# RWKV triangles beside the projections, 32x32 blocks inverted on GpSimd, decay in the transposes

## The reference

```python
def step(state, inp):
    r_t, w_t, k_t, v_t, av_t, bv_t = inp
    sa = jnp.einsum('bhvk,bhk->bhv', state, av_t)
    state = (state * w_t[:, :, None, :] + sa[..., None] * bv_t[:, :, None, :]
             + v_t[..., None] * k_t[:, :, None, :])
    return state, jnp.einsum('bhvk,bhk->bhv', state, r_t)
...
_, y = lax.scan(step, s0, xs)
```

## Time and profile before

| | us |
|---|---|
| median of 3 runs | 3227.96 (3223.63 to 3230.2) |
| the profiled execution | 3227.73 |
| its span, first to last instruction | 3226.4 |
| PE busy | 3011.9 (93%) |
| DVE busy | 1792.1 (56%) |
| ACT busy | 1269.2 (39%) |
| POOL busy | 69.0 (2%) |

### The profile page before, as it was taken

The page is one execution under the profiler, slowest core; times in us unless marked ns, Lnnn a source line. Parts: engine busy times, 40 slices in busy tenths (PEclk is TensorE's granted clock), DMA queues, the critical chain, the costliest instruction groups (busy, mean ns, idle before and its releaser), DMA issues. The chain is left out here.

```text
span 3226.4 us, 65777 instructions
## 1 busy us (share of the span) xinstructions
PE 3011.9 (93%) x27928; PEld 2412.8 (75%) x27928; DVE 1792.1 (56%) x3385; ACT 1269.2 (39%) x2310; POOL 69.0 (2%) x36
## 2 busy tenths in 40 slices
PE   8998999999988999999999999898989899999998
PEld 6666777766667777767777777788878887778876
DVE  3566566523475245565654565556666665453465
ACT  4354343321244455555544444322222225443233
POOL 0000000000000001111100000000000000000000
PEclk9998999999999999999999999999999999999999
DMA  3000111242145522223233423431212225431114
GB/s 116 20 20 27 40 46 53 66 147 80 61 124 157 159 57 78 74 74 80 72 80 111 137 85 132 160 128 36 80 32 90 75 75 202 137 116 52 33 59 150
DMA packets 143972, 284.23 MB, mean 88 GB/s; under 512 B 43312, under 2 KB 84288, under 8 KB 142144
## 3 DMA queue, kind: packets, MB, share of 16 engines
q1 hardware_dynamic: 143680, 280.04, 27.5%
HBM read 222.79 MB, written 57.21 MB: 87 GB/s over the span
## 5 line engine op out<-in xcount | busy, mean ns | idle before, releaser
L234 PE MATMUL ps<-xs,wparts 128*128 128x512 f32 x1664 | 694.3, 417 | 12.0 <-DVE xs L1494 9.5
L236 PE MATMUL ps<-xs,wparts 128*128 128x512 f32 x1664 | 654.0, 393 | 0.0
L235 PE MATMUL ps<-xs,wparts 128*128 128x512 f32 x1664 | 652.8, 392 | 0.0
L302 DVE TENSOR_TENSOR wparts<-wring,wparts 128x1024 fp32r<-128x1024 f32 x248 | 303.9, 1225 | 311.7 <-ACT wparts L294 286.8
L234 PEld LDWEIGHTS ps<-xs,wparts 128*128 128x128 f32 x1664 | 313.3, 188 | 126.1 <-issue 63.7
L294 ACT ACTIVATE wparts<-wring 128x1024 fp32r<-128x1024 f32 x248 | 263.1, 1061 | 276.9 <-PE ps L236 214.3
L236 PEld LDWEIGHTS ps<-xs,wparts 128*128 128x128 f32 x1664 | 312.6, 188 | 71.2
L235 PEld LDWEIGHTS ps<-xs,wparts 128*128 128x128 f32 x1664 | 313.8, 189 | 60.7 <-issue 4.5
L2271 ACT ACTIVATE Pm<-Pm,ml 128x128 f32<-128x128 f32 (+1 forms) x384 | 168.4, 441 | 147.9 <-DVE ml L2339 147.8
L2339 DVE CUSTOM_DVE_ANT_0 Pm<-ps,mask 128x128 f32<-128x128 f32 (+1 forms) x384 | 110.8, 347 | 186.7 <-PE ps L2174 186.7
L2647 ACT ACTIVATE M<-ps 128x256 f32<-128x256 f32 x160 | 61.5, 384 | 258.5 <-PE ps L2446 249.9
(11 more groups left out here) (400 smaller groups left out, 5407.8 us busy)
## 6 DMA issues: line engine op xcount, KB each, us to landing
wring<-in_wo SPq DMA_DIRECT2D x96, 512.0 KB, 3.6
ops<-rw SPq DMA_DIRECT2D x32, 640.0 KB, 6.1
wring<-in_w SPq DMA_DIRECT2D x39, 512.0 KB, 3.5
wring<-in_w2u SPq DMA_DIRECT2D x33, 512.0 KB, 4.2
wring<-in_wg SPq DMA_DIRECT2D x24, 512.0 KB, 3.6
wring<-in_w2v SPq DMA_DIRECT2D x24, 512.0 KB, 4.2
wring<-in_w2a SPq DMA_DIRECT2D x24, 512.0 KB, 6.4
MB<-wst SPq DMA_DIRECT2D x48, 256.0 KB, 5.1
```

The source lines that it names most:

```text
L234: nc.tensor.matmul(out, a, c, start=start, stop=False)
L235: nc.tensor.matmul(out, b, c, start=False, stop=False)
L236: return nc.tensor.matmul(out, a, d, start=False, stop=stop)
L302: K.nc.vector.tensor_tensor(W.part(i, 1), W.raw(i), W.part(i, 0).bitcast(F32), ALU.subtract).then_inc(*K.dve.done("w_lo", W.first + i))
```

## The change

1. **The triangle Bc x AR moves into the projections.** `triangles_pe` does it for pair p-1 beside the units of the next group, four quarters q of 16 products each, three rounds apart; `triangles_dve` masks each quarter into one buffer `mbs`, and `mb_store` on SP writes it to DRAM ("mx"). The DVE instruction of a quarter waits until the store of the quarter before has landed. The last pair's four quarters come behind the units.
2. **GpSimd inverts the 32x32 diagonal blocks.** `solve_move` on SP gathers the 64 blocks of a pair into 64 partitions by four DMAs (runs of 128 bytes). `solve_pool` does 30 steps, each a multiplication and an addition over s x (31-s) elements. `xt_store` writes the inverses back by four DMAs. `solve_move` of pair p first waits for POOL's pair p-1 and stores it. Pairs 0 to 5 have it behind the weight loads 13, 17, 21, 25, 29 and 32; pair 6 between the first loads of the recurrence and the last `prep_store`; pair 7 inside the recurrence. A load of a piece needs its pair's `xt_store`.
3. **PE keeps one corner.** Per piece and stream, instead of five levels there are eight 32x32 products (`m1_mm`), two short ACT copies, eight more (`xt_mm`), a DVE transpose (`x11`) and one masked DVE copy of 128x128.
4. **The decay goes into the turns.** Kc and Bc are turned with a diagonal dg that holds the decay (four ACT instructions of 128x64), so L2768 goes and the state takes one instruction.
5. **The rounds.** Each piece has twelve rounds for chain and stage, the second stream's stage a round later, and `finish` is spread over four pieces.

```diff
     for p in range(NP):
         for i in range(4 * p + 3 if p else 6, 4 * p + 7):
             if i < 33:
                 yield from w_load(K, B.W, i)
+            if i in MB_AT:
+                yield from mb_store(K, A, B, MB_AT.index(i))
+            if i in SOLVE_AT:
+                yield from solve_move(K, A, B, SOLVE_AT.index(i))
         if p:
             yield from prep_store(K, A, B, p - 1)
+    yield from mb_store(K, A, B, NP - 2)
     yield from rwkv_first_sp(K, A, B.rw)
+    yield from solve_move(K, A, B, NP - 2)
     yield from prep_store(K, A, B, NP - 1)
+    yield from mb_store(K, A, B, NP - 1)
+    sp.wait_ge(*(yield "mb_store", NP - 1, 3))
     for p in (NP - 2, NP - 1):
         sp.wait_ge(*(yield "rw_store", p, "b"))
     barrier(K, sp, 3)
...
+MB_AT, SOLVE_AT = [12, 16, 20, 24, 28, 31], [13, 17, 21, 25, 29, 32]
+def mb_store(K, A, B, p):
+    for q in range(4):
+        K.sp.wait_ge(*(yield "m_b", p, q))
+        if p == 0 and q == 0:
+            K.sp.wait_ge(*(yield "mb_zero"))
+        K.nc.sync.dma_start(A["mx"][p][:, 4 * q:4 * q + 4, :], B.mbs).then_inc(*K.sp.done("mb_store", p, q, by=16))
...
+def xt_store(K, A, B, p):
+    K.sp.wait_ge(*(yield "solved", p))
+    for i, here, there in corners(A, B, p, 128):
+        K.nc.sync.dma_start(there, here).then_inc(
+            *K.sp.done("xt_part", p, i, by=16, also=[("xt_store", p)] if i == 3 else []))
+def solve_move(K, A, B, p):
+    K.sp.wait_ge(*(yield "mb_store", p, 3))
+    if p:
+        yield from xt_store(K, A, B, p - 1)
+        K.sp.wait_ge(*(yield "xt_store", p - 1))
+    for i, here, there in corners(A, B, p, 0):
+        K.nc.sync.dma_start(here, there).then_inc(
+            *K.sp.done("g_part", p, i, by=16, also=[("g_load", p)] if i == 3 else []))
...
+    G = B.G[0:64, :].rearrange("p (i t) -> p i t", t=32)
+    pool.wait_ge(*(yield "g_load", p))
+    pool.in_order()
+    nc.gpsimd.memset(B.G[0:64, 0:1024:33], 1.0).then_inc(*pool.done("one_diag", p))
+    for s in range(1, 31):
+        n = 31 - s
+        d = B.tmp[0:64, 0:s * n].rearrange("p (i t) -> p i t", t=n)
+        pool.in_order()
+        nc.gpsimd.tensor_tensor(d, G[:, 0:s, s:s + 1].to_broadcast([64, s, n]),
+                                G[:, s:s + 1, s + 1:32].to_broadcast([64, s, n]), ALU.mult).then_inc(
+            *pool.done("step_mul", p, s))
+        pool.in_order()
+        nc.gpsimd.tensor_tensor(G[:, 0:s, s + 1:32], G[:, 0:s, s + 1:32], d, ALU.add).then_inc(
+            *pool.done("step_add", p, s, also=[("solved", p)] if s == 30 else []))
...
+    for q in range(4):
+        bank, old = B.RM.take(("mb_mm", p, q), ("m_b", p, q))
+        pe.wait_ge(*(yield "prep", p))
+        pe.wait_ge(*(yield old))
+        for c in range(4 * q, 4 * q + 4):
+            a = tiles(nc, bank[:, half(c % 4, 128)], Bc[:, c, :], AR[:, c, :])
+        a.then_inc(*pe.done("mb_mm", p, q))
+        for _ in range(3):
+            yield STEP
...
+def triangles_dve(K, B, p):
+    nc, dve = K.nc, K.dve
+    for q in range(4):
+        dve.wait_ge(*(yield "mb_mm", p, q))
+        if q:
+            dve.wait_ge(*(yield "mb_store", p, q - 1))
+        elif p:
+            dve.wait_ge(*(yield "mb_store", p - 1, 3))
+        else:
+            dve.wait_ge(*(yield "mar"))
+        dve.in_order()
+        nc.vector.tensor_tensor(B.mbs[:, :, 0:128], K.bank["mb_mm", p, q].rearrange("p (c t) -> p c t", c=4),
+                                B.mar[:, :].unsqueeze(1).to_broadcast([128, 4, 128]), ALU.mult).then_inc(
+            *dve.done("m_b", p, q))
+        for _ in range(3):
+            yield STEP
...
+    gens = [in_turn(*[exactly(ROUNDS, chain(K, B, s, n)) for n in range(4 * NJ)]) for s in range(2)]
+    gens += [in_turn(*[exactly(ROUNDS, later(s, stage(K, B, s, n))) for n in range(1, 4 * NJ)]) for s in range(2)]
+    gens += [later(4 * ROUNDS, in_turn(*[exactly(4 * ROUNDS, later(2 * s, finish(K, B, s, j, SPREAD)))
+                                         for j in range(NJ - 1)])) for s in range(2)]
+    if split:
+        gens.append(later(3 * ROUNDS + 1, in_turn(*[exactly(ROUNDS, split(K, B, k)) for k in range(8, 16)])))
+    yield from weave(*gens)
...
-            if j and n == 4 * j + ND:
-                for s in range(2):
-                    yield from fin_store(K, A, B, s, j - 1)
+            yield from ops_load(K, A, B, s, n)
+        if n == 4:
+            yield from solve_move(K, A, B.prep, NP - 1)
+        if n == 8:
+            yield from xt_store(K, A, B.prep, NP - 1)
+            K.sp.wait_ge(*(yield "xt_store", NP - 1))
+            yield from mix_load(K, A, B, 15)
+        if n in (10, 14):
+            yield from finished_sp(K, A, B, n // 4 - 2)
+    yield from finished_sp(K, A, B, NJ - 2)
...
+    LT, _, XT = triangles(B, s, n)
+    XM = B.XM[:, s]
+    bank, old = B.RG.take(("mk_mm", s, n), ("m_k", s, n))
+    if old:
+        pe.wait_ge(*(yield old))
+    for c in range(4):
+        a = tiles(nc, bank[:, half(c, 128)], K4[:, c, :], AR[:, c, :])
+    a.then_inc(*pe.done("mk_mm", s, n))
+    yield STEP
+    yield STEP
+    bank, old = B.RG.take(("side_t", s, n, 0), ("side", s, n, 0))
+    if old:
+        pe.wait_ge(*(yield old))
+    turned(K, B, bank, V4, lambda c: B.stack).then_inc(*pe.done("side_t", s, n, 0))
+    yield STEP
+    yield STEP
+    bank, old = B.RG.take(("m1_mm", s, n), ("m1", s, n))
+    pe.wait_ge(*(yield "x11", s, n))
+    if old:
+        pe.wait_ge(*(yield old))
+    for c in range(4):
+        a = corner(nc, bank[:, half(c, 32)], LT[:, c, 32:64], XM[:, c, :], 0)
+    a.then_inc(*pe.done("m1_mm", s, n))
+    yield STEP
+    yield STEP
+    for x, src in ((1, K4), (2, B4)):
+        bank, old = B.RG.take(("side_t", s, n, x), ("side", s, n, x))
+        pe.wait_ge(*(yield "dg", s, n))
+        turned(K, B, bank, src, lambda c: B.dg[:, s, c, :]).then_inc(*pe.done("side_t", s, n, x))
+        if x == 1:
+            yield STEP
+            yield STEP
+            bank, old = B.RG.take(("xt_mm", s, n), ("xt", s, n))
+            pe.wait_ge(*(yield "m1", s, n))
+            if old:
+                pe.wait_ge(*(yield old))
+            for c in range(4):
+                a = corner(nc, bank[:, half(c, 32)], XM[:, c, :], XT[:, c, 32:64], 1)
+            a.then_inc(*pe.done("xt_mm", s, n))
+            yield STEP
+            yield STEP
...
+    dve.wait_ge(*(yield "ops_load", s, n))
+    dve.in_order()
+    nc.vector.transpose(XM[:, :, :], XT[:, :, 0:32]).then_inc(*dve.done("x11", s, n))
...
-        dve.wait_ge(*(yield state_key(s, n, c)))
-        dve.in_order()
-        nc.vector.tensor_scalar(d, B.ST[:, s, i, :], pc, None, ALU.mult).then_inc(*dve.done("r_decay", s, n, c))
...
-        nc.vector.scalar_tensor_tensor(B.ST[:, s, 1 - i, :], K.bank["w_mm", s, n, c][:, 0:64], pc, d, ALU.mult,
-                                       ALU.add).then_inc(*dve.done("r_state", s, n, c))
-        yield STEP
```

More of the change, by code:

```diff
@@ L214, in drive, with exactly @@
         assert moved, [asked[e] for e in live]
+def exactly(n, gen):
+    done = 0
+    x = next(gen, None)
+    while x is not None:
+        if x is STEP:
+            done += 1
+            yield STEP
+            x = next(gen, None)
+        else:
+            v = yield x
+            try:
+                x = gen.send(v)
+            except StopIteration:
+                x = None
+    assert done <= n, (done, n)
+    for _ in range(n - done):
+        yield STEP
 def later(steps, gen):
@@ L2630, in rwkv_first_pe @@
     K.pe.wait_ge(*(yield "c2c"))
-    yield from weave(*[stage_pe(K, B, s, 0) for s in range(2)], steps=True)
+    yield from weave(*[later(s, stage_pe(K, B, s, 0)) for s in range(2)], steps=True)
 def rwkv_pe(K, A, B):
@@ L2667, in chain_act @@
     j, g = divmod(n, 4)
-    for _ in range(12):
+    for _ in range(ROUNDS):
         yield STEP
@@ L2688, in finish_act @@
         *act.done("y_sq", s, j))
-    for _ in range(3):
+    for _ in range(sum(at[2:4])):
         yield STEP
@@ L2789, in finish_dve, with rounds @@
     bc = lambda x: x.unsqueeze(2).to_broadcast([128, 16, 64])
-    for _ in range(s):
-        yield STEP
+    def rounds(*which):
+        for _ in range(sum(at[i] for i in which)):
+            yield STEP
+    yield from rounds(0)
     dve.wait_ge(*(yield "y_out", s, 4 * j + 3))
```

318 lines of the change are left out of this document (162 added, 156 removed).

## The result

The changed kernel takes 3073.1 us (median of 4 runs, 3068.8 to 3085.3) against 3227.8 for the kernel before. The ratio is 0.9528, with a 95% interval of 0.9499 to 0.9558, so it is 4.7% faster. The forecast was 3097, in a range of 3010 to 3200. The profiled execution, the shortest of the four, took 3068.8 us, and its span is 3067.4, 159.0 us shorter than before.

The account below looks back on a forecast made before the run. The recurrence was taken as bounded by PE's instruction count, DVE's big instructions second. 3226.4 + 56 (projections) + 31 (transition) - 217 (recurrence) = 3096, with 1.3 us around the span 3097; range 3010 to 3200.

Parts of the forecast that it names:

- its own case: Whole kernel: the predicted costs and gain hold as summed, 3097 us, within 3050 to 3150; chance 0.50.
- Projections: Seven projection groups: each pays 4.9 us of PE's triangle work and 3.1 us waiting on DVE, +56 us (44 to 80).
- Transition: Last unit to barrier: POOL's pair 5, stores, gathering and pair 7's four round trips in SP's queue, +31 us (+12 to +60).
- Recurrence: Recurrence: 246 us of PE's records and shape changes plus 79 us of other things, 325 for 542.5, -217 us.
- PE's own output: Recurrence: PE's records take 225 us for 431, and 60 shape changes at 0.35 us add 21, making 246 us.
- The rest: Recurrence: what is left of 111 us beyond PE's output, from finishes, ACT's copy, loads, clock and others, 79 us.
- The finishes at 26 us: Recurrence: DVE's 1.2 us finish instructions in rounds of 1.2 us cost some 2.2 us a piece for twelve pieces, 26 us.
- ACT's copy of Y: Recurrence: the copy comes behind the second stream's last turned copy, so PE waits about 0.9 us a piece, 13 us.
- The stalls stay: Recurrence: rival that all 111 us beyond PE's output remain, since DVE works in order; total 3129 us; chance 0.14.
- POOL paces: Solves: rival that from 52 us a solve they fall behind the groups; at 60 us, total about 3185; chance 0.15.
- slower: SP's queue ahead of the barrier: rival that solves from 67 us erase the gain; at 80 us, about 3304; chance 0.09.
- The shared port pair: POOL's solves: contending two-input DVE instructions add 10 us to a solve of 44; without that, the result is 11 us lower.

Follow-up runs that it names:

- the run with one step of thirty: The changed kernel with GpSimd doing one step of the thirty in each solve, so the inverses are not the reference's: 3067.5 us, ratio 0.9505.
- the new transition: The changed kernel with stage 0 woven with the last pair's quarters, third pieces' loads behind the quarters' stores, wait for pair 5 behind the barrier: 3057.6 us.

## Why the prediction was right, and where not

The time lay 24 us below the forecast, inside its own case (3050 to 3150). The recurrence's gain, which decides it, came out as forecast in its sum. That was luck in part: two errors of 18 us cancelled. The two costs had the right sign and were a third and nearly a half smaller. By its steps:

- **Projections, +56 forecast, +37 measured.** PE's share was right. In PE's timeline of a quarter the second product behind it starts 1.68 us after the last before it, so 4 x (0.86 + 0.35) = 4.9 us a group, and the group grew by 5.0. The step that failed is DVE's wait for the store, 3.1 us a group. I took 5 us for a store of 384 KB from the earlier trace rows. It lands in 2.3 (median):

```profile
mx<-early SPq DMA_DIRECT2D x32, 384.0 KB, 2.3
```

  Two quarters follow each other in 3.07 us where I had 6.1. The first store of a group, behind a weight load, takes 4.2 to 6.5 us, and only for it did my 5 hold. D was ready 0.3 to 2.4 us ahead of PE in all groups but the last, where PE waited 1.7 us. Seven times 3.1 less that wait is 20 us, about this term's error of 19. The rows that I took were medians of other transfers of 512 KB in a busier queue.
- **Transition, +31 forecast, +17 measured.** Pair 5 was solved 17.7 us after the first piece's load (24 forecast, with a longer group), and from there to the barrier it took 34.4 us, not 42. Storing, gathering and the six stores took 11.7 us where I had 17.7. The four round trips took 16.1 us to the last landing, not 24: the first, behind the six stores, 6.9, and each other store 2.3. Then came 6.6 us of stage 0, which I had at nothing, as hidden. DVE makes its masks behind the fourth quarter. That the barrier waits for POOL was so in SP's queue, but not in the time. With the solves cut to 2 us the barrier stayed where it was. With the wait, the store and the gather moved behind it, it came 7 us earlier and the time stayed. Reordering the queue and DVE gained 15.5.
- **Recurrence, -217 forecast and measured, with two terms off in opposite directions.** PE's own output: 480 x 54 ns, 960 corner records at 23 ns and 5,916 others at 28.9 make 219 us, and 60 changes of shape at 0.15 are 9: 228, where I had 246. The switch of 0.35 us from the earlier trace rows, between 128-row and 64x64 products, does not hold between 64 and 32. The rest was 97 us, not 79: 57 us of idle PE and 40 us in which it was slower (busy 268 for 228). The clock explains about half of the 40. It was at its lower level for 47.8 us, as long as in the recurrence before. By the estimate above, some 18 us were lost there (31 ns is 228 us over 7,356 records), for which I had 20. The other 22 lie at the full clock, and what they are stays open. The finishes at 26 us were near: cut to a sixteenth of their columns they gave 14 to 24. ACT's copy of Y had 13 and measured 8.6.
- **Rivals.** "The stalls stay" (111 us) was nearer than its chance of 0.14 says: 97 us for all that isn't output lies nearer to it than to my 79. "POOL paces" and "slower" did not happen, but the run with a longer solve came to 3176.5 us with its first six solves at 59 to 69 us, 65 on average (3185 forecast for P = 60). So the mechanism was right and its rule too steep: the groups were 3 us shorter, and 7.9 us lie between two solves then, not 14. Its threshold of 52 us did not follow from my own pitch (58 less 14 is 44); from the measured ones it is about 47.
- **The shared port pair.** The Trainium skill says in SBUF — State Buffer, Who interferes with whom, that a DVE instruction with two inputs in SBUF contends with a GpSimd instruction that reads SBUF. GpSimd's 2.46 us, from just behind the start of DVE's scan to just behind its end, agree with it. I had 10 us a solve for it, and the solves bear that out: 34.4 us for pair 6, where DVE was busy for 9.8 of them, and 42.4 for pair 0, where it was busy for 21.3. In the kernel's time the run with one step of thirty shows some 6 us for all of GpSimd's work by the medians, where I had 11 for this alone.

What stays open: how much of the 15.5 us of the new transition belongs to which of its three edits, what sets the granted clock in the recurrence, and what slows PE there at the full clock. The tail's +4.2 us was not looked into; it lay between 589 and 600 us in the profiles of kernels with the same tail.

## What to carry to other kernels

Count an engine's instructions at their measured spacing first: that gave the recurrence's gain, and was off by 8% of PE's sum. Price a round trip through DRAM from a transfer of its own kind in its own queue, and when an engine's wait is taken out of a barrier's way, look what stands second there (here a store behind some 9 MB, and a stage behind four round trips), since that was worth more. Where a chain alternates between two engines, spread the second's big instructions once. Here a second spreading gave nothing, and less work for that engine did. And when a sum comes out right, compare its terms: here two of them were 18 us off.
